# Expert weights loaded with eight neighbouring rows per partition in one piece, and the transposes before them reordered to match

## The reference

```python
def routed_moe(x, router_w, router_b, w_gate, w_up, w_down):
    ...
    for e in range(N_EXPERTS):
        h = jax.nn.silu(xt @ w_gate[e]) * (xt @ w_up[e])
        y = y + gates[:, e:e + 1] * (h @ w_down[e])
```

## Time and profile before

| | |
|---|---|
| median of 3 runs | 2032.33 us (2021.67 to 2037.64) |
| the profiled execution, its own time | 2042.54 us |
| its span (first to last instruction) | 2040.9 us |
| TensorE busy | 1919.4 us (94%) |
| VectorE, ScalarE, GpSimd busy | 655.7, 409.1, 84.9 us |
| mean granted TensorE clock | 0.962 of full speed |
| the two expert parts on TensorE | about 1120 to 1414 us and 1726 to 2017 us |

### The profile page before, as it was taken

One profiled execution on the slowest core, in us unless ns is written; L12 is line 12 of the kernel. 1 busy time (PEld: TensorE's weight loads), 2 busy tenths in 40 slices (PEclk: granted clock), 3 DMA queues, 4 the chain that ended last, 5 costly groups with the idle time before them and its releaser, 6 DMA issues.

```text
span 2040.9 us, 23060 instructions
## 1 busy us (share of the span) xinstructions
PE 1919.4 (94%) x9698; PEld 867.5 (43%) x9698; DVE 655.7 (32%) x1579; ACT 409.1 (20%) x874; POOL 84.9 (4%) x107
## 2 busy tenths in 40 slices
PE   6999999999999999999996999999899996999997
PEld 3464444444444444544645333323544644333332
DVE  3746232223310044013725100003598645100005
ACT  4203011111100003203801111111326701111112
POOL 0000100000000000000000200001000000200001
PEclk9989999999999999998996999999998996999999
DMA  4202922122221113101044699998112053899994
GB/s 148 77 21 78 364 83 72 52 83 72 83 72 62 62 55 124 57 26 42 1 155 157 232 386 396 397 386 316 42 42 83 1 185 134 275 399 396 396 389 176
DMA packets 143752, 335.68 MB, mean 164 GB/s; under 512 B 6632, under 2 KB 15864, under 8 KB 143520
## 3 DMA queue, kind: packets, MB, share of 16 engines
q1 hardware_dynamic: 129504, 283.91, 38.0%
q0 software_dynamic: 10976, 37.78, 4.9%
q10 hardware_dynamic: 3168, 12.50, 1.5%
HBM read 311.07 MB, written 23.09 MB: 164 GB/s over the span
## 4 chain that ended last, share of the span: by engine, by line
PE 86%; DMA 6%; DVE 5%; ACT 2%; issue 1%; DVEq 0%; SPq 0%; ACTq 0%
PE psum L608 38%; PE psum L1042 22%; PE psum L879 7%; DMA ring<-in_moe_w_up 5%; PE psum L812 5%; PE psum L954 3%; PE psum L983 2%; PE psum L967 2%; PE psum L1136 1%; PE psum L1023 1%; PE psum L754 1%; PE psum L620 1%; ACT ring L1495 1%; PE psum L1198 1%; PE psum L1067 1%
## 5 line engine op out<-in xcount | busy, mean ns | idle before, releaser
L1042 PE MATMUL psum<-ring,scratch 128*32 128x512 f32 x3840 | 525.9, 603 | 15.8 <-DMA ring<-in_moe_w_up 10.0
L608 PE MATMUL psum<-xT,ring 128*128 128x512 f32 (+2 forms) x1136 | 457.5, 563 | 14.2 <-DVE xT L1726 4.5
L608 PEld LDWEIGHTS psum<-xT,ring 128*128 128x128 f32 x1136 | 209.4, 193 | 257.8 <-issue 247.5
L1042 PEld LDWEIGHTS psum<-ring,scratch 128*32 128x32 f32 x3840 | 146.7, 111 | 308.4 <-issue 303.9
L608 PE MATMUL psum<-ring,xT 128*128 128x512 f32 (+2 forms) x576 | 223.3, 546 | 2.5 <-ACTq L1248 1.6
L879 PE MATMUL psum<-ring,scratch 128*128 128x512 f32 x352 | 152.7, 593 | 1.8 <-PE psum L879 1.5
L608 PEld LDWEIGHTS psum<-ring,xT 128*128 128x128 f32 x576 | 103.9, 190 | 118.6 <-issue 110.4
L1667 DVE SCALAR_TENSOR_TENSOR scratch<-psum,overlay,scratch 128x511 f32<-128x511 f32 x88 | 65.9, 749 | 222.3 <-ACT scratch L1427 220.7
L1042 PE MATMUL psum<-xT,scratch 128*32 128x512 f32 x768 | 130.3, 607 | 7.5 <-DMA ring<-in_moe_w_up 7.5
L2202 DVE TENSOR_TENSOR scratch<-psum,scratch 128x512 f32<-128x512 f32 x24 | 16.6, 692 | 350.4 <-PE psum L1042 314.5
L812 PE MATMUL psum<-xT,ring 128*128 128x512 f32 x224 | 101.4, 608 | 2.4 <-DVEq L1656 2.3
(11 more groups left out here) (376 smaller groups left out, 1621.2 us busy)
## 6 DMA issues: line engine op xcount, KB each, us to landing
ring<-in_moe_w_gate SPq DMA_DIRECT2D x28, 2048.0 KB, 15.5
ring<-in_moe_w_up SPq DMA_DIRECT2D x28, 2048.0 KB, 17.5
ring<-in_moe_w_down SPq DMA_DIRECT2D x24, 2048.0 KB, 14.7
ring<-in_w_up SPq DMA_DIRECT2D x11, 2048.0 KB, 8.9
xT<-in_moe_w_down SPq DMA_DIRECT2D x8, 2048.0 KB
expert_rows<-scratch ACTq DMA_DIRECT2D x20, 512.0 KB, 7.5
ring<-in_w_down SPq DMA_DIRECT2D x4, 2048.0 KB, 8.1
ring<-in_even_w_in SPq DMA_DIRECT2D x4, 2048.0 KB, 8.3
```

What stands on the lines that cost most here:

```text
L608: mm = nc.tensor.matmul(out_, lhsT, rhs, start=(j == 0), stop=(j == len(pairs) - 1))
L1042: mm = nc.tensor.matmul(bank[r, :], lhsT[:, t, r], w_[:, t, c0:c0 + 512], start=(t == 0), stop=(t == nk - 1))
```

## The change

The view of the expert matrices becomes `e (p k) n -> e p (k n)`. Partition p now holds rows 8p to 8p+7 of a gate or up matrix (4p to 4p+3 of a down matrix), which are neighbours in memory, in one piece of 16 KB. Step t of a product then uses row 8p + t of the matrix on partition p, so the transposed tokens must have column 8p + t on partition p in step t. `turn_x` therefore takes every eighth column of the gathered rows, beginning at t, where it took 128 neighbouring ones, and `turn_h` every fourth of `hid`. The products themselves, their number and their order stay.

```diff
             def turn_x(l, g):
+
+                of_partition = xg[:, g % 2, :].rearrange("q (p k) -> q k p", k=KD)
                 pe.wait_ge(gathered[g % 2], 16 * (NG // 2 * l + g // 2 + 1))
                 for h in range(2):
                     for t in range(4):
-                        mm = nc.tensor.transpose(banks[h][:, t * P:(t + 1) * P],
-                                                 xg[:, g % 2, (4 * h + t) * P:(4 * h + t + 1) * P], ident)
+                        mm = nc.tensor.transpose(banks[h][:, t * P:(t + 1) * P], of_partition[:, 4 * h + t, :], ident)
                     mm.then_inc(xgT_done, 1)
...
             def turn_h(l, g):
+                of_partition = hid.rearrange("q (p k) -> q k p", k=4)
                 pe.wait_ge(h_ready, NG * l + g + 1)
                 for t in range(4):
-                    mm = nc.tensor.transpose(banks[4][:, t * P:(t + 1) * P], hid[:, t * P:(t + 1) * P], ident)
+                    mm = nc.tensor.transpose(banks[4][:, t * P:(t + 1) * P], of_partition[:, t, :], ident)
                 mm.then_inc(hT_done, 1)
...
             def load_experts(l):
                 c0 = first_expert_chunk[l]
-                views = {m: w[n][l].rearrange("e (k p) n -> e p k n", p=P) for m, n in zip(("gate", "up", "down"), EXPERT_W)}
+                views = {m: w[n][l].rearrange("e (p k) n -> e p (k n)", p=P) for m, n in zip(("gate", "up", "down"), EXPERT_W)}
...
-                    sp.dma_start(expert_buffer(b, 4 if m == "down" else KD), views[m][e]).then_inc(w_loaded[b], 16)
+
+                    sp.dma_start(expert_buffer(b, 1)[:, 0, :], views[m][e]).then_inc(w_loaded[b], 16)
```

## The result

The changed kernel takes **2006.47 us** in the median (2005.87 to 2011.59, 4 runs) against 2032.38 us: ratio **0.988**, 95% interval 0.9846 to 0.9913. Repeated twice beside the kernel before, it gave 0.9898 (0.9881 to 0.9914) and 0.9876 (0.9857 to 0.9894). It is faster by a little over 1%, where I had forecast 0.2% slower.

A forecast was written before the change was run, and what follows sets the result against it. The prediction took transfers as the bound, with TensorE only 3 to 4 us a cycle behind. Faster loads (-24.2 us) and dearer transposes (+28.6 us) made +4.4 us on the 2032.3 us median: 2037 us, range 2006 to 2070 us.

The forecast's parts named there:

- rival B: Strided loads of the transposes in turn_x and turn_h are free, 0.118 us for 128 columns; 2008 to 2014 us; chance 0.25.
- What bounds the kernel: In the expert parts transfers set the pace; TensorE's waits (17.5 us) and low clock behind them (6.7 us) cost 24.2 us.
- The loads: Expert matrices in 16 KB pieces move at 427 GB/s, a cycle's transfers take 66.3 us, below TensorE's 67.67 us.
- The transposes: Strided loads in turn_x and turn_h take 0.236 us each, 1.19 us more a group, 28.6 us in 24 groups.
- C: Only the wide stride of turn_x costs, 0.83 us a group, turn_h nothing; -4 us, 2028 us; chance 0.12.
- D: Strides of 32 and 16 bytes in the transposes hit the same few banks, 3.5 us a group; 2093 us; chance 0.18.
- the faster side: The whole kernel becomes faster by over 1%, mostly the case of free strides; chance 0.20.
- The sum: Over the whole run, -24.2 + 28.6 = +4.4 us, which applied to the median of 2032.3 us gives 2037 us.

The follow-up runs named there:

- The loads alone: The changed kernel with both transposes put back to neighbouring columns; 2015.66 us, ratio 0.9879 to the kernel before.
- half the bytes: The kernel before, transferring only the first half of each expert matrix from the eighth load of a layer on; 2013.11 us, ratio 0.9875.
- experiment on L754: L754 loading one half of the partitions at step 33 in the first block, both halves from neighbouring columns in the second; 0.118 us a stepped load, neighbouring half.
- experiment on a product's step: The changed kernel with gate and up products loading 32 stationary columns at a step of 8 elements; median load 137 ns instead of 110.
- gate and up alone: The changed kernel with down put back to old 4 KB pieces and plain transposes; 2018.2 us, ratio 0.9895 to the kernel before.

## Why the prediction was wrong

I forecast +4.4 us and measured -25.9. The stated range of 2006 to 2070 us holds the 2006.47 us only by half a microsecond, at the end that rival B had given it.

**What bounds the kernel: right.** The transfers were the bound, and 24.2 us is what they cost within the noise. The loads alone gave 24.1 us and half the bytes 26.7 (ratios 0.9879 and 0.9875, each to 0.002).

**The loads: right in what they did.** They became fast enough, packets hold a whole piece, TensorE became the bound with 67.9 us a cycle, and no wait took the old one's place. The forecast 427 GB/s stood for a share of 1.04; the loads alone ran at 425 with a share of 1.01, which is 421 for a share of one where I had taken 411. That the two raw figures are so near is luck, and the forecast transfer cycle of 66.3 us was never seen by itself, since TensorE set the pace. The Trainium skill's rule of a fixed cost for each packet ("DMA: Bandwidth & Descriptors", "Why small descriptors are slow (HBM only)") gives a gain of 5%, an estimate from that page. The windows of before and of the loads alone show 397 and 425 GB/s, 7%, or 10% for equal shares (382 and 421). The packet records of the weights' queue in the traces of before and after agree with the larger figure: a packet of 2 KB lasts 84 ns in the median, one of 4 KB 159 ns, one of 16 KB 611 ns, so eight of 2 KB take 672 ns for the same bytes.

**The transposes: wrong, and this is the step that failed.** I wrote that a strided load of a transpose costs "1.84 ns for each of 128 columns, 0.236 us, and then sets the pace", 28.6 us in all. It costs 0.15 us for a group, 3.6 us in all. The row for L754 was read rightly (experiment on L754), and a product's load at step 8 pays about as much (experiment on a product's step), but a transpose's load is another kind. It takes 142 ns for 128 columns where a product's takes 190, 0.4 ns a column less, and at a step 196 to 210 ns. How that stays hidden can only be estimated. A product's loads of 32 and 128 neighbouring columns take 112 and 190 ns, 0.8 ns a column on a fixed 86 ns; with the same fixed part a stepped transpose comes to (196 - 86) / 128 = 0.86 ns a column, 0.11 us for 128 columns, just about as long as the 0.11 us that stream past. The row of the right kind stood in the same group, though not at a step; I named the difference as a point for rival B and then priced by the row that was alike in step and not in kind.

**The rivals.** B's time came, but for a small miss: 2008 to 2014 us forecast, 2006.47 measured, and on the first result's scale the two repeats make 2011.6 and 2007.1. It came with a price near B's 0.118 us for 128 columns, but not for B's reason: L754's pair does not share a path. C fell: turn_x pays 0.06 us for a group and not 0.83, and steps of 2 to 5 elements cost as much as 8. The rule of the Trainium skill behind it ("SBUF — State Buffer", "Door 1: The DMA port swizzle"), that up to 4 fp32 are free, is not what these traces show for a weight load: step 2 already takes 209 ns where neighbouring columns take 147, and step 4 in turn_h has a longer load than step 8 in turn_x, 210 against 196 ns. D fell, as no step up to 31 is dear. I had given B 0.25 and the faster side 0.20, too little for a case whose only obstacle was a row of another kind.

**The sum.** -24.2 + 3.6 = -20.6 us; the three comparisons gave -25.9, -21.3 and -23.1 us. All three are a little larger than the sum, and the interval of the third (-29.1 to -21.5 us) just leaves it out, so some 1 to 5 us may be missing in it; which term, no run shows. The profiles differ by 36.0 us: 20.6 of the sum and 12.7 of the short gaps, which the one had and the other had not, leave 2.7 us unexplained.

## What to carry to other kernels

When a kernel's two bounds lie 3 us in 70 apart, find the amount that the slower one costs (its waits, and the lower clock behind them): that is the ceiling of any edit to it, and half the edit may already reach it, as gate and up alone did here. Price a changed access by a row of the same kind of instruction first, and of the same step only then; where the kinds differ, take their ratio from rows that show both. Before a difference of two profiles is explained, look whether a repeat of one of them shows it too.

## What the runs showed of the hardware

- A transpose's weight load of 128 fp32 columns takes 142 to 147 ns for neighbouring columns and 194 to 234 ns at steps of 2 to 31 elements, with no growth with the step, and least at 8, 16 and 24. Eight in a row slow from 1.03 us to between 1.09 and 1.28 us.
- A product's load pays about twice as much for a step: 0.84 ns a column more at step 8, and 1.85 ns a column in all at step 33 where neighbouring columns take half. Two loads for different halves of the partitions run side by side.
- At a step the duration of a product's load does not follow the granted clock: L754's loads take 209 ns at a granted clock of 1.00 and at 0.50 alike. Neighbouring columns do: 128 of them, from the same tensor `at_rank`, take 192 ns at 1.00 (L1076) and 330 ns at 0.50 (L1015), both in the kernel before.
- On the weights' queue a packet of 2 KB lasts 84 ns in the median, 4 KB 159 ns, 16 KB 611 ns; a piece of 16 KB is one packet. With such pieces a window moves 425 GB/s where 2 and 4 KB pieces move 397.
- VectorE's product of a PSUM and an SBUF operand, 128x512, slowed from 692 to 1121 ns when both were read at a step of 4.
- Short gaps under "issue" in the same places of the program, which cost a place 1.7 to 4.3 us, are present in every profile of two batches and absent in every profile of a third, on the same chip as one of the two. What they are stays open.
